# Two row halves side by side in one 512-column product, their sum moved to VectorE

## What is computed

```
q = (xc @ w_q).reshape(-1, PEER_HEADS, 2, half)
...
g = jax.nn.softmax(cv, axis=-1)
...
a = jax.nn.gelu(jnp.einsum('td,thkd->thk', xc, ue)).astype(jnp.float32)
return jnp.einsum('thk,thkd->td', (g * a).astype(ve.dtype), ve)
```

```
def swiglu(x, w_gate, w_up, w_down):
    return (jax.nn.silu(x @ w_gate) * (x @ w_up)) @ w_down
```

## Time and profile before

| | |
|---|---|
| time, median of 3 runs (lowest, highest) | 3311.08 us (3308.05, 3312.18) |
| the profiled execution: its time, its span | 3311.66 us, 3309.9 us |
| PE, PEld busy | 3208.4 us (97%), 2865.0 us (87%) |
| DVE busy | 2380.8 us (72%) |
| ACT, POOL busy | 1663.3 us (50%), 480.4 us (15%) |
| read from memory | 576.96 MB, 175 GB/s over the span |

### The profile page before, as it was taken

How to read it: one execution, slowest core, us unless ns; L and a number is a source line. 1 busy time by engine, 2 the same in 40 slices (tenths; PEclk the granted TensorE clock), 3 DMA queues, 4 the chain that set the end, 5 groups by cost and what they waited for, 6 DMA issues and landing times.

```text
span 3309.9 us, 57249 instructions
## 1 busy us (share of the span) xinstructions
PE 3208.4 (97%) x22739; PEld 2865.0 (87%) x22739; DVE 2380.8 (72%) x4014; ACT 1663.3 (50%) x2679; POOL 480.4 (15%) x361
## 2 busy tenths in 40 slices
PE   6999999999998889999999999999999999999999
PEld 6789977889888669987799999989879999888798
DVE  7879989777767569999966556558775555687754
ACT  3455555444444464555545444446654444565543
POOL 1168100000000257500000000001140000022300
PEclk9999999999999899999999999999999999999999
DMA  9445455677766225545566665655336555544455
GB/s 329 164 135 181 147 163 170 197 254 239 257 198 229 83 66 172 167 146 172 169 207 217 183 186 171 183 175 169 120 121 185 185 176 184 173 145 140 128 183 167
DMA packets 160535, 582.26 MB, mean 176 GB/s; under 512 B 18448, under 2 KB 20240, under 8 KB 160144
## 3 DMA queue, kind: packets, MB, share of 16 engines
q1 hardware_dynamic: 156528, 569.69, 54.8%
q10 hardware_dynamic: 3168, 8.35, 0.7%
q0 software_dynamic: 576, 0.57, 0.1%
HBM read 576.96 MB, written 1.05 MB: 175 GB/s over the span
## 4 chain that ended last, share of the span: by engine, by line
PE 87%; DVE 7%; DMA 2%; ACT 2%; issue 1%; POOL 1%; ACTq 0%; DVEq 0%; POOLq 0%
PE P L807 22%; PE P L1976 22%; PE P L1999 21%; PE P L858 12%; PE P L1962 2%; DVE LOW L522 1%; DVE ssd_a L2801 1%; PE P L787 1%; PE P L825 1%; PE P L883 1%; DMA RING<-in_pu 1%; DVE mix_a L574 1%; PE P L790 1%; PE P L1054 1%; PE P L795 0%
## 5 line engine op out<-in xcount | busy, mean ns | idle before, releaser
L522 DVE TENSOR_TENSOR LOW<-RING,HI 128x1024 fp32r<-128x1024 f32 x884 | 1075.9, 1227 | 378.9 <-ACT HI L509 378.0
L509 ACT ACTIVATE HI<-RING 128x1024 fp32r<-128x1024 f32 x988 | 1034.1, 1053 | 378.4 <-DMA RING<-in_pu 152.9
L807 PE MATMUL P<-HTH,HI 128*128 128x256 f32 x2240 | 325.5, 288 | 10.8 <-ACT HI L509 5.9
L807 PE MATMUL P<-HTH,LOW 128*128 128x256 f32 x2240 | 317.4, 285 | 7.0 <-DVE LOW L522 7.0
L807 PE MATMUL P<-HTL,HI 128*128 128x256 f32 x2240 | 316.7, 284 | 0.0
L807 PEld LDWEIGHTS P<-HTH,HI 128*128 128x128 f32 x2240 | 292.0, 193 | 21.4 <-issue 10.7
L1976 PE MATMUL P<-HTH,HI 128*128 128x256 f32 x2048 | 298.9, 285 | 1.6 <-ACT HI L509 1.5
L807 PEld LDWEIGHTS P<-HTH,LOW 128*128 128x128 f32 x2240 | 290.3, 193 | 9.7 <-DVE LOW L522 9.6
L807 PEld LDWEIGHTS P<-HTL,HI 128*128 128x128 f32 x2240 | 291.3, 193 | 0.0
L1976 PE MATMUL P<-HTL,HI 128*128 128x256 f32 x2048 | 289.1, 284 | 0.0
L1976 PE MATMUL P<-HTH,LOW 128*128 128x256 f32 x2048 | 287.5, 283 | 0.0
(11 more groups left out here) (436 smaller groups left out, 5035.2 us busy)
## 6 DMA issues: line engine op xcount, KB each, us to landing
RING<-in_pu SPq DMA_DIRECT2D x256, 512.0 KB, 3.6
RING<-in_pv SPq DMA_DIRECT2D x256, 512.0 KB, 3.6
RING<-in_ada SPq DMA_DIRECT2D x64, 512.0 KB, 4.7
RING<-in_fgA SPq DMA_DIRECT2D x44, 512.0 KB, 3.6
RING<-in_fuA SPq DMA_DIRECT2D x44, 512.0 KB, 3.6
RING<-in_fdA SPq DMA_DIRECT2D x44, 512.0 KB, 3.6
RING<-in_fgB SPq DMA_DIRECT2D x44, 512.0 KB, 3.6
RING<-in_fuB SPq DMA_DIRECT2D x44, 512.0 KB, 3.6
```

The source lines that it names most:

```text
L509: act.activation(c.his[i % NHL], c.raw[m % NR], ACT.Copy).then_inc(*c.hi.at(("hi", m)))
L522: eng.tensor_tensor(c.low[m % NR], c.raw[m % NR], c.his[i % NHL].bitcast(F32), ALU.subtract).then_inc(*sig.at(("lo", m)))
L807: m = pe.matmul(ps[:, 0:256], w[:, k * 128:k * 128 + 128], c.ht[h][:, k, :], start=i == 0 and k == 0, stop=i == 2 and k == 7)
```

## The change

The two halves of the stage input become one buffer `HT`, so that a single moving operand can take slice k of both, 2 x 256 columns. A new `project_halves` runs 8 matmuls of 512 columns (both halves with `HI`) and then 8 of 256 columns (`HTH` with `LOW`, into the first half of the bank). The bank then holds two partial sums, and a new `halves_vector` on VectorE adds them with one TENSOR_REDUCE into SBUF. This is done for the gate and up tiles of the four ffn stages and for the up tiles from block 64 on of the two peer stages. `project_two` in the ffn stages keeps its matmuls but puts the `HTL` part into the second half of the bank, so that the first two tiles can be read in the same way. ScalarE's silu and gelu now read what the reduce wrote. In the late part of peer, ScalarE makes the next down tile's high half ahead of the gelu instead of behind it.

```diff
+        self.both = sbuf("HT", 4096, F32R)[:, :].rearrange("p (h k t) -> p h k t", h=2, k=8)
+        self.ht = [self.both[:, h, :, :] for h in range(2)]
...
+def project_halves(pe, c, name, j):
+
+    n, hi, lo = c.tile(name, j)
+    ps = open_bank(pe, c, name, j)
+    pe.wait_ge(*c.by("hi", n))
+    for k in range(8):
+        pe.matmul(ps, hi[:, k * 128:k * 128 + 128], c.both[:, :, k, :], start=k == 0, stop=False)
+    pe.wait_ge(*c.by("lo", n))
+    for k in range(8):
+        m = pe.matmul(ps[:, 0:256], lo[:, k * 128:k * 128 + 128], c.ht[0][:, k, :], start=False, stop=k == 7)
+    m.then_inc(*c.pe.at(("used", n), ("product", name, j)))
+
+
+def halves_vector(dve, c, name, j, dst, event):
+
+    dve.wait_ge(*c.by("product", name, j))
+    ps = c.psum(name, j).rearrange("p (h t) -> p t h", h=2)
+    dve.tensor_reduce(dst, ps, AX.X, ALU.add).then_inc(*c.dve.at(event, ("free", name, j)))
...
     for j in range(64, 130):
         if j < 128:
-            peer_up_tensor(pe, c, f, j, ())
+            project_halves(pe, c, f.u, j)
...
 def peer_up_scalar(act, c, f, j):
+    if j >= 64:
+        act.wait_ge(*c.by(f.s, "up", j))
+        act.activation(f.act_of(c, j), f.act_of(c, j), ACT.Gelu_apprx_tanh).then_inc(*c.act.at((f.s, "gelu", j)))
+        return
...
+        if j >= 66:
+            feed(act, c, "act", f.v, j - 2)
         if j < 128:
             peer_up_scalar(act, c, f, j)
         if j >= 66:
-            feed(act, c, "act", f.v, j - 2)
...
         if 65 <= j < 129:
             peer_rest_vector(dve, c, f, j - 1)
+        if j < 128:
+            dve.wait_ge(*c.by(s, *(("weighed_lo", j - 4) if j >= 68 else ("weighed", 63))))
+            halves_vector(dve, c, f.u, j, f.act_of(c, j), (s, "up", j))
         if j >= 66:
             modulation_vector(dve, c, (f.v, j - 2))
...
-    project_two(pe, c, s, [(f.g, 0), (f.u, 0)])
+    project_two(pe, c, s, [(f.g, 0), (f.u, 0)], 256)
     for j in range(1, 22):
-        project(pe, c, f.g, j)
-        project(pe, c, f.u, j)
+        project_halves(pe, c, f.g, j)
+        project_halves(pe, c, f.u, j)
...
         feed(dve, c, "dve", f.g, j)
+        if j >= 2:
+            dve.wait_ge(*c.by(s, "hidden_lo", j - 2))
+        halves_vector(dve, c, f.g, j, f.sg[j % 2], (s, "gate", j))
         feed(dve, c, "dve", f.u, j)
-        dve.wait_ge(*c.by("product", f.u, j))
+        halves_vector(dve, c, f.u, j, f.su, (s, "up", j))
+        dve.wait_ge(*c.by(s, "up", j))
         dve.wait_ge(*c.by(s, "silu", j))
-        dve.tensor_tensor(f.sg[j % 2], c.psum(f.u, j)[:, 0:256], f.sg[j % 2], ALU.mult).then_inc(
-            *c.dve.at((s, "gated", j), ("free", f.u, j)))
+        dve.tensor_tensor(f.sg[j % 2], f.su, f.sg[j % 2], ALU.mult).then_inc(*c.dve.at((s, "gated", j)))
```

More of the change, by code:

```diff
@@ L378, in __init__ @@
         self.x = sbuf("X", 2048)[:, :].rearrange("p (t n) -> p t n", t=2)
-        self.ht = [sbuf(n, 2048, F32R)[:, :].rearrange("p (k t) -> p k t", k=8) for n in ("HTH", "HTL")]
+        self.both = sbuf("HT", 4096, F32R)[:, :].rearrange("p (h k t) -> p h k t", h=2, k=8)
+        self.ht = [self.both[:, h, :, :] for h in range(2)]
         with ExitStack() as shared:
@@ L775, in norm_vector, with project_two @@
                     *c.dve.at((s, "htl", k)))
-def project_two(pe, c, s, tiles):
+def project_two(pe, c, s, tiles, at=0):
     places = [c.tile(*x) for x in tiles]
@@ L789, in project_two @@
         for k in range(8):
-            pe.matmul(o[:, 0:256], lo[:, k * 128:k * 128 + 128], c.ht[0][:, k, :], start=False, stop=False)
+            pe.matmul(o[:, 0:256], lo[:, k * 128:k * 128 + 128], c.ht[0][:, k, :], start=False, stop=at > 0 and k == 7)
     for (n, hi, lo), o, x in zip(places, ps, tiles):
@@ L794, in project_two @@
                 pe.wait_ge(*c.by(s, "htl", k))
-            m = pe.matmul(o[:, 0:256], hi[:, k * 128:k * 128 + 128], c.ht[1][:, k, :], start=False, stop=k == 7)
+            m = pe.matmul(o[:, at:at + 256], hi[:, k * 128:k * 128 + 128], c.ht[1][:, k, :], start=at > 0 and k == 0,
+                          stop=k == 7)
         m.then_inc(*c.pe.at(("used", n), ("product", *x)))
@@ L2349, in __init__ @@
         self.sg = [c.at(s, T00 + 256 * n, 256) for n in range(2)]
+        self.su = c.at(s, T00 + 512, 256)
         self.scale = c.const(f"fn{'1' if s[3] == 'A' else '2'}_{s[4]}")
@@ L2377, in ffn_scalar @@
         feed(act, c, "act", f.g, j)
[L2378 to L2382, removed]
+        act.wait_ge(*c.by(s, "gate", j))
+        act.activation(f.sg[j % 2], f.sg[j % 2], ACT.Silu).then_inc(*c.act.at((s, "silu", j)))
         feed(act, c, "act", f.u, j)
```

## The result

The changed kernel took 3275.49 us in the median (3274.25 to 3282.07, 4 runs) against 3310.73 us of the kernel before in the same comparison. The ratio is 0.9893, interval 0.9880 to 0.9906. So the change saves 30 to 35 us.

A forecast was written before the change was run, and what follows sets the result against it. The prediction took TensorE to be the bound, without a gap in ffn and only just in late peer0; 22 us saved by joined products less 2.5 us given back in peer0 made -19.5 us, 3291.5 us, range 3280 to 3305.

The forecast's parts named there:

- The bound and the mechanism: Whole kernel: TensorE, 97% busy, is the bound; joining two 256-column matmuls into one of 512 saves 8 to 11 ns.
- The price of a joined product: TensorE, ffn and late peer: 229 to 232 ns per 512-column product, against 240 ns for two of 256.
- the worth of the join: 168 ffn tiles save 10.8 us and 128 late peer tiles 11.3 us, sum 22 us, all on the path.
- The rival with 237.5 ns a joined product: Joined tiles: only a small fixed cost is saved, 6 us, giving 3305 us; chance 0.04.
- The reduce: VectorE, once a tile: 0.67 us, hidden behind TensorE in ffn.
- The slow case (1.31 us): Reduce at 1.31 us makes VectorE the bound: ffn +54 us, peer0 about +8, total about 3366; chance 0.09.
- my point of decision: In ffn, VectorE becomes the bound once a reduce takes 0.91 us.
- part 3: Late peer: VectorE's reduce stays hidden in peer1 but crowds peer0, where the ACC step and next pv transfer come later.
- 2.5 us given back: Peer0's late part: the reduce delays the transfer loop, costing 0.06 us a pair over 40 pairs.
- the margin: Peer0: pv's high half is ready 0.95 us before TensorE wants it; reduce and shorter up tiles leave 0.2 us.
- ScalarE's moved step: Late peer: making the pv high half ahead of gelu keeps the loop free of gelu's reduce; no size given.
- what the profile after would show: Joined starts 229 to 232 ns apart, ffnA0 2.8 us shorter, peer1 pairs 5.56 us, peer0 high-half waits 3.6 to 6 us.

The follow-up runs named there:

- split: The changed kernel with each joined 512-column product made two of 256 again, reduce, waits and moved ScalarE step kept: 3310.35 us, ratio 0.9996 to the kernel before.
- reduce_twice: The changed kernel with every VectorE reduce done twice, same output: 3350.33 us, ratio 1.0118 to the kernel before.
- again: The changed kernel without any edit, profiled and timed a second time: 3278.56 us, ratio 0.9909 to the kernel before.
- peer_only: The kernel before with the change only in the late part of the two peer stages, ScalarE's order included, ffn as before: 3293.30 us, ratio 0.9947.
- spacer: The kernel before with one idle VectorE operation ahead of the background step into ACC in late peer pairs: 3306.78 us, ratio 0.9984.

## Why the prediction was wrong

**The bound and the mechanism** were right. TensorE bounds both kernels; split shows that without the join there is no gain.

**The price of a joined product** was right within 2 ns (230 measured, 229 to 232 taken), the worth of the join a little low: 14.5 us in ffn where I had 10.8, since I priced ffn by its down tiles (232 ns). Peer1 gained 6.3 where I had 5.6. In place of 22 us these tiles gave 14.5 + 2 x 6.3 = 27.1, by 0.086 us a tile in ffn and 0.10 a pair in peer. This is a mis-sized term, by 5 us. The rival with 237.5 ns a joined product would have made 6 us of these 27.

**The reduce** costs 688 ns, against 670 taken, and is hidden as said. The slow case (1.31 us) did not come; reduce_twice, at 1.38 us, shows that it would have decided the sign, and puts my point of decision low by a tenth.

**The step that failed is part 3**, "2.5 us given back" in peer0. Its two profiles in the changed kernel and again gave 8.8 and 10.7 us in place of the 3.1 that 5.6 less 2.5 had left, and peer_only 12.4. I had taken the `pv` transfer's later start at the price of the margin it uses up, and on top expected it to be slower because it then starts beside the `ada` transfer. It got faster: 4.4 to 3.6 us. The pair that answers to the earlier trace rows in again, whose up tile starts at 824.96 us:

```profile
827.49 0.33 SPq L532 DMA_DIRECT2D RING<-in_pv  x1
...
830.66 1.06 ACT L510 ACTIVATE HI<-RING 128x1024 fp32r<-128x1024 f32 x1 [0.99 <-DMA RING<-in_pv]
...
833.28 1.07 PE L2021 MATMUL P<-HI,peer_wh_latex 128*128 128x512 f32 x4
```

The transfer starts 2.53 us into the pair in place of 2.08 and is with ScalarE 3.17 us later in place of 4.42. The high half is there at 831.72, 1.56 us before TensorE wants it. I had counted 0.95 us down to 0.2; it grew instead. I looked at the transfer that follows and not at the one that is still under way. Nor did I ask what the kernel before lost there already: in some pairs a high half had waited for a slow transfer. Eleven of its pairs took over 0.1 us more than the usual one, against 7 in the changed kernel and 4 in again, and the sum fell from 7.2 us to 3.9 and 2.8. So 2.5 us given back were 3.3 to 4.4 us gained.

**Neither error alone** would have brought the time out of the range: 5 us of the join leave 3286, 6 to 7 us of peer0 3285. Together, with up to 3 us of clock, they make the 13 to 16 us by which the medians lie below 3291.5.

**ScalarE's moved step** was rightly said to keep the loop free of the reduce. What I did not do is give it a price: beside the reduce it is 12 to 14 us. Without it the change would have given 18 us, nearly what I forecast for the whole; that would have been luck, since peer0 would then have gained nothing at all.

**What the sum left out** is 0.3 (first profile) and 2.9 us (again) of clock in the ssd stages (last section) and up to 3 us, of either sign, in mix0 and mix1.

Of what the profile after would show: joined products at 229 to 232 ns, held (230); ffnA0 2.8 us shorter, 3.6 came; no idle of TensorE in ffn, held; peer1's pairs at 5.56 us, 5.53 came; waits for ScalarE's high half in peer0 up from 3.6 us to 6, refuted (2.0 us in the changed kernel and 1.4 in again over the same 740 to 990 us).

**What stays open.** The sign of the later start is the same in every profile and in both edits that move it. Its size is not settled: by the sums over pairs it is 1 to 6 us in peer0, and the kernels of one side differ by 2 to 3 among themselves. The timed runs give 2 to 9 us for spacer, most of which its profile has outside of peer0, and under 5 for split, down to nothing. Whether the `pv` transfer gets faster because the `pu` one is out of its way, or for another reason that goes with the start, was argued from the landing times and not tried by itself.

## What to carry to other kernels

Where TensorE is the bound without a gap, look at the distance of starts for each shape: two products that share their weights are worth joining if the wide one starts less than twice as far from the next as the narrow one (here 230 against 240 ns, 0.086 us a tile, 296 tiles), and if another engine has the room for the sum that is then left over. When an edit puts an operation ahead of a step that frees a buffer, don't only subtract it from the margin: ask which transfer the next one will now miss, as it may land sooner, and look at its time to landing before you price the delay. And price the small reordering that comes with a large edit by itself; here it was over a third of the gain.

## What was not expected of the hardware

**A transfer that started half a microsecond later landed 0.8 us sooner after its start** (4.4 to 3.6 us in the median), so that it was there earlier all the same. A kernel with an idle operation of 0.70 us on VectorE in each late pair was faster by 0.16% (0.06% to 0.26%), though its profile has only 1.7 of 6.6 us of that in the stage where the transfers are tight.

**The ssd stages, unchanged, came out 1.5 us shorter or 1.2 us longer with the clock.** Stretches of ssd0 in the kernel before, then in again: us, busy time of PE, PEld, DVE, ACT, POOL, granted clock, DMA share, GB/s.

```profile
2355.70:2359.10 3.40, 1.37 (x11) 1.37 (x12) 3.33 (x5) 2.55 (x10) 0.00 (x0) 1.00 0.50 154
2359.10:2362.50 3.40, 3.40 (x19) 3.40 (x17) 3.30 (x6) 0.31 (x2) 0.00 (x0) 0.50 0.00 0
```

```profile
2333.00:2336.40 3.40, 1.41 (x11) 1.41 (x12) 3.32 (x5) 2.52 (x9) 0.00 (x0) 1.00 0.48 154
2336.40:2339.80 3.40, 3.40 (x31) 3.40 (x30) 3.31 (x5) 1.57 (x3) 0.00 (x0) 1.00 0.19 46
```

In both TensorE was busy for only 1.4 us of the stretch ahead. In the kernel before the granted clock then stood at half (1.2 GHz) for the next stretch, with 19 matmuls in it; in again it stayed at 2.4 GHz, with 31. The same instructions with the same pause, 134 us behind the start of ssd0 in both, are throttled in one execution and not in the other; what I see differ is when they come. The kernel before has one such stretch in each ssd stage, again has none. The whole times of ssd0 fall on two levels over all twelve profiles, 253.2 us with such a stretch and 251.7 without. In ssd1 the changed kernel has one as the kernel before has, but 0.9 us earlier in the stage, and takes 254.3 us in place of 253.1. The Trainium skill ("TensorE: Matmul & The Clock Gate", section What's actually happening) says that the chip's own count runs freely and does not begin with the kernel; the two executions agree with that.
